# Expert weights of a hybrid decoder layer: two 1 MB pieces of one matrix by one 2 MB transfer

## The chip, the cores and the metric

The kernel runs on one core of one Trainium2 chip. The metric is the device time of one execution in microseconds. TensorE multiplies, ScalarE and VectorE work element by element, GpSimd (POOL) issues the gathers and scatters, SyncE (SP) issues the other transfers. Each engine runs its own instructions in program order and waits on semaphores.

## The reference, cut to what matters

One decoder layer on 1024 tokens of width 1024: a combined projection, differential attention and retention, a gated merge, an output projection, and a mixture of 32 SwiGLU experts of which each token uses two. The change touches the experts alone:

```
h2 = rms_norm(x, norm2_g)                       # (1024, 1024)
for each expert e (width 512), on the rows routed to it:
    a = rows @ w_gate[e]                        # w_gate, w_up: (32, 1024, 512) float32
    u = rows @ w_up[e]
    y = (silu(a) * u) @ w_down[e]               # w_down: (32, 512, 1024) float32
    out[rows] += y * routing weight
```

The three matrices of an expert have 2 MB each, so the experts read 201 MB of weights.

## The kernel before

The stages ahead of the experts end at about 890 us. In the expert stage each expert works on one block of 128 gathered rows. All products are made as three products of parts (`split3`): each float32 operand is taken apart into a high part in float32r and the low rest. ScalarE makes the high part of a weight piece (`high_piece`, L1167), VectorE the low part (`low_piece`, L1703), and both are needed before TensorE can use the piece.

**Pieces and ring.** Each matrix of an expert comes in two pieces of 1 MB, 128 partitions with 8 KB each. So an expert has 6 pieces: c = 0 to 3 for gate and up, c = 4 and 5 for down. `PIECES` puts the 192 pieces in the order of use: the four pieces of expert e stand ahead of the two down pieces of expert e - 1. Gate and up alternate: gate first half, up first half, gate second half, up second half. The pieces go through a ring of 10 slots of 16 KB per partition, of which the loaded piece fills the first 8 KB (the low part replaces it there) and the high part the other 8 KB. Each slot has a semaphore `w_land0` to `w_land9` for the landing. `load_piece` on SP waits until the piece that was in the slot ten pieces earlier is used:

```
if q >= N_SLOTS:
    sp.wait_ge(S["w_used"], q - N_SLOTS + 1)
```

TensorE raises `w_used` after the 12 matmuls of each piece (`gate_up`, `down`). The loads are all issued on SP, first pieces 0 to 3 amid the stores of the stage before, then the others in one loop once the first expert's rows have landed.

**Order on the engines**, for expert e (the 32 experts in order of use, `expert_at` says which one it is):

- TensorE: four pieces of gate and up for e; turn the rows of expert e + 1 (`turn_x`, L562); two down pieces of e - 1; turn the hidden rows of e (L562).
- ScalarE: silu of e (`gate_silu`, L1180); high part of the next rows (`x_high`, L1171); high parts of pieces (e + 1, 1) and (e + 1, 2); high part of the turned hidden rows (L1175); high parts of (e + 1, 3), (e, 4), (e, 5) and (e + 2, 0).
- VectorE: hidden rows of e, silu times up (`hidden`, L1779); low part of (e + 1, 0); low part of the next rows (`x_low`, L1774); low part of (e + 1, 1); the weighed result y of e - 1 (`rows_out`, L1800); low part of the hidden rows (L1783); low parts of (e + 1, 2), (e + 1, 3), (e, 4) and (e, 5).
- GpSimd: gather the rows of expert e + 3 when those of e + 2 are turned (L1335); scatter y of expert e with an addition in memory (L1343).

PSUM holds gate's product in `PROJ[0]`, up's in `PROJ[1]`. `overflow` and its blocks serve experts with more than 128 rows.

## Time and profile before

| | before |
|---|---|
| median of 3 runs | 1505.51 us (1505.3 to 1505.54) |
| the profiled execution | 1504.28 us |
| its span, first to last instruction | 1502.3 us |
| TensorE busy, share of the span | 1431.3 us, 95% |
| VectorE busy | 1015.5 us, 68% |
| ScalarE busy | 768.6 us, 51% |
| GpSimd busy | 387.9 us, 26% |
| transfers | 282.68 MB, mean 188 GB/s |
| mean granted TensorE clock, share of full speed | 0.988 |

The profile is of one execution. Times count from the first instruction's start. Busy shares are averages over stages that differ, so the expert stage has to be looked at by itself, by windows, timelines and the chain of waits, which follows the work that ended last back from step to step. In timelines a merged row (xN) covers all its instructions from the first start to the last end.

### The profile page before, as it was taken

How to read it: one execution, taken by the hardware profiler on the slowest of the kernel's cores; microseconds unless marked ns; L12 is line 12 of the kernel's file. 1: busy time of each engine (PE TensorE's matmuls, PEld its weight loads, DVE VectorE, ACT ScalarE, POOL GpSimd, SP SyncE). 2: the span in 40 equal slices, each digit the busy share in tenths (PEclk: the TensorE clock that was granted, in tenths of full speed). 3: DMA queues.
4: the chain of work that ended last, by engine and by line, in shares of the span. 5: the costliest groups of instructions: out<-in, count | busy, mean ns of one | idle time of the engine just before them, and what ended most of it. 6: DMA issues, size and time to landing. Idle time of an engine off the chain costs nothing.

```text
span 1502.3 us, 19200 instructions
## 1 busy us (share of the span) xinstructions
PE 1431.3 (95%) x7296; PEld 1198.4 (80%) x7297; DVE 1015.5 (68%) x1433; ACT 768.6 (51%) x1091; POOL 387.9 (26%) x448
## 2 busy tenths in 40 slices
PE   5899999999999999999999969999999999999995
PEld 4788888888888788888888858888888787777784
DVE  6855655664664433434332876999999999999994
ACT  5643453453453322333232446767777777777772
POOL 2325325424424300000001421333332222222221
PEclk9999999999999999999999979999999999999998
DMA  7011010110210333453341469999999999999991
GB/s 227 13 43 45 17 43 11 51 42 2 60 43 1 85 84 89 122 144 85 84 189 57 169 234 377 362 373 376 375 378 375 374 367 364 367 370 368 365 347 49
DMA packets 129996, 282.68 MB, mean 188 GB/s; under 512 B 15728, under 2 KB 94704, under 8 KB 105328
## 3 DMA queue, kind: packets, MB, share of 16 engines
q1 hardware_dynamic: 119216, 264.31, 48.8%
q0 software_dynamic: 9216, 16.81, 4.5%
q8 instruction: 60, 0.98, 0.3%
q10 hardware_dynamic: 1472, 0.32, 0.1%
q14 instruction: 32, 0.26, 0.1%
HBM read 273.00 MB, written 25.17 MB: 198 GB/s over the span
## 4 chain that ended last, share of the span: by engine, by line
PE 72%; DMA 14%; DVE 6%; issue 2%; ACT 2%; POOL 2%; POOLq 0%; DVEq 0%; ACTq 0%
PE proj L105 14%; PE proj L107 14%; PE proj L106 13%; DMA w_slot<-in_w_up 9%; PE scores L105 5%; PE scores L107 5%; PE scores L106 5%; DMA w_slot<-in_w_gate 4%; PE outs L751 2%; PE scores L684 2%; DVE w_low L1703 2%; ACT w_high L1167 1%; PE turned L105 1%; PE turned L107 1%; PE turned L106 1%
## 5 line engine op out<-in xcount | busy, mean ns | idle before, releaser
L1703 DVE TENSOR_TENSOR w_low<-w_slot,w_high 128x2048 fp32r<-128x2048 f32 x192 | 434.4, 2285 | 11.1 <-ACT w_high L1167 10.0
L1167 ACT ACTIVATE w_high<-w_slot 128x2048 fp32r<-128x2048 f32 x190 | 359.6, 1914 | 106.7 <-DMA w_slot<-in_w_gate 40.8
L105 PE MATMUL proj<-w_high,xeH 128*128 128x512 f32 x512 | 206.2, 403 | 11.5 <-DVE w_low L1703 8.7
L107 PE MATMUL proj<-w_high,xeL 128*128 128x512 f32 x512 | 201.3, 393 | 0.0
L106 PE MATMUL proj<-w_low,xeH 128*128 128x512 f32 x512 | 201.2, 393 | 0.0
L1343 POOL DMA_INDIRECT out<-y,ids_rows x32 | 107.1, 3347 | 228.9 <-DVE y L1800 228.9
L105 PEld LDWEIGHTS proj<-w_high,xeH 128*128 128x128 f32 x512 | 97.2, 190 | 38.9 <-DVE w_low L1703 16.3
L975 ACT ACTIVATE wCH<-wC_in 128x1024 fp32r<-128x1024 f32 x48 | 47.6, 1052 | 154.4 <-DMA wC_in<-in_w_branch_b 154.4
L1398 DVE TENSOR_TENSOR wCL<-wC_in,wCH 128x1024 fp32r<-128x1024 f32 x48 | 56.9, 1237 | 91.3 <-ACT wCH L975 91.3
L107 PEld LDWEIGHTS proj<-w_high,xeL 128*128 128x128 f32 x512 | 97.1, 190 | 21.3
L1335 POOL DMA_INDIRECT xe<-h_rows,ids_rows x32 | 54.8, 1711 | 225.9 <-PE scores L562 213.4
L106 PEld LDWEIGHTS proj<-w_low,xeH 128*128 128x128 f32 x512 | 97.2, 190 | 18.9
L105 PE MATMUL proj<-wBH,hTH 128*128 128x512 f32 x256 | 111.5, 436 | 0.0
L105 PE MATMUL scores<-w_high,hidH 128*128 128x512 f32 x256 | 103.4, 404 | 4.9 <-DVE w_low L1703 4.9
L105 PE MATMUL proj<-wAH,hTH 128*128 128x384 f32 x256 | 97.7, 382 | 5.7 <-DVE wAL L1393 4.2
L107 PE MATMUL proj<-wBH,hTL 128*128 128x512 f32 x256 | 101.1, 395 | 0.0
L107 PE MATMUL scores<-w_high,hidL 128*128 128x512 f32 x256 | 100.5, 393 | 0.0
L106 PE MATMUL proj<-wBL,hTH 128*128 128x512 f32 x256 | 100.3, 392 | 0.0
L106 PE MATMUL scores<-w_low,hidH 128*128 128x512 f32 x256 | 100.2, 391 | 0.0
L107 PE MATMUL proj<-wAH,hTL 128*128 128x384 f32 x256 | 86.5, 338 | 0.0
L106 PE MATMUL proj<-wAL,hTH 128*128 128x384 f32 x256 | 86.2, 337 | 0.0
L105 PEld LDWEIGHTS scores<-w_high,hidH 128*128 128x128 f32 x256 | 48.6, 190 | 14.1 <-issue 5.1
(277 smaller groups left out, 3080.5 us busy)
## 6 DMA issues: line engine op xcount, KB each, us to landing
w_slot<-in_w_gate SPq DMA_DIRECT2D x64, 1024.0 KB, 21.1
w_slot<-in_w_up SPq DMA_DIRECT2D x64, 1024.0 KB, 22.2
w_slot<-in_w_down SPq DMA_DIRECT2D x64, 1024.0 KB, 21.1
wC_in<-in_w_in SPq DMA_DIRECT2D x32, 512.0 KB, 4.9
wB_in<-in_w_in SPq DMA_DIRECT2D x16, 512.0 KB, 6.4
wA_in<-in_w_in SPq DMA_DIRECT2D x12, 512.0 KB, 5.8
x_all<-in_x SPq DMA_DIRECT2D x4, 1024.0 KB, 8.7
wC_in<-in_w_branch_a SPq DMA_DIRECT2D x16, 256.0 KB, 5.6
```

Source lines behind the costliest of these rows:

```text
L105: pe.matmul(out, lh, rh, start=start, stop=False)
L106: pe.matmul(out, lh, rl, start=False, stop=False)
L107: return pe.matmul(out, ll, rh, start=False, stop=stop)
L684: pe.matmul(SC[:, c, t0 * 128:t1 * 128], q_part[r, 0, :], k_part[r, 1 + t0:1 + t1, :].rearrange("p a b -> p (a b)"), start=q_part is qkTH ...
L751: last = pe.matmul(OB[:, 0:128], aT[:, j, :], V[:, j, :], start=(j == 0), stop=(j == i2))
L975: act.activation(wCH[sub][:, piece * 8:piece * 8 + 8, :], wC_in[sub][:, piece * 8:piece * 8 + 8, :], ACT.Copy).then_inc(S["wC_high"], 1)
L1167: act.activation(w_high[slot][:], w_in6[slot][:], ACT.Copy).then_inc(S["w_split"], 1)
L1335: pool.indirect_dma_start(out=xe[:], out_offset=None, in_=h2_dram, in_offset=bass.IndirectOffsetOnAxis(ap=ids_rows[:, expert_at(j):expert_ ...
L1343: pool.indirect_dma_start(out=out_rows, out_offset=bass.IndirectOffsetOnAxis(ap=ids_rows[:, expert_at(j):expert_at(j) + 1], axis=0), in_=y ...
L1398: dve.tensor_tensor(wCL[sub][:, r, :], wC_in[sub][:, r, :], wCH[sub][:, r, :].bitcast(F32), ALU.subtract).then_inc(S["wC_low"], 1)
L1703: dve.tensor_tensor(w_low[slot][:], w_in6[slot][:], w_high[slot][:].bitcast(F32), ALU.subtract).then_inc(S["w_lows"], 1)
```

## The change

The order of use within an expert becomes gate, gate, up, up, down, down, so that neighbouring pieces are the two halves of one matrix. Where such a pair lies in slots 0 and 1, 4 and 5, 6 and 7 or 8 and 9, `load_pair` issues one transfer of 2 MB: 128 partitions, per partition 16 KB in a row of the source, put down as two runs of 8 KB that lie 16 KB apart. It waits until both slots are used. Both halves then have one semaphore, so the high part of either half waits for both. Slots 2 and 3 (`ALONE`) don't lie side by side, and there the pair stays two transfers of 1 MB. To make the other slots neighbours, slots 3 to 7 get other places in memory. Pieces 0 and 1, loaded ahead, are one pair; 2 and 3 are loaded one by one at the places where they were. As gate is whole after piece 1, `gate_silu` waits for piece 1 instead of 3, and `hidden` waits for piece 3 itself. For expert 0, whose rows come in two halves, the second half is wanted at piece 1 instead of 2.

```diff
--- before.py
+++ after.py
@@ -36,6 +36,8 @@
 NO_ROW = 1024
 N_SLOTS = 10
 N_GROUPS = 4
+ALONE = (2, 3)
+BLOCK_SLOTS = (0, 1, 2, 4, 5, 6)
 
 
 def expert_at(j):
@@ -48,6 +50,11 @@
     if c < 4:
         return max(6 * e - 2, 0) + c
     return min(6 * e + 8, 6 * N_EXP - 2) + c - 4
+
+
+def land_of(slot):
+
+    return f"w_land{slot if slot in ALONE else slot - slot % 2}"
 
 
 PIECES = sorted((use_of(e, c), e, c) for e in range(N_EXP) for c in range(6))
@@ -318,9 +325,11 @@
         key_w = [ro(f"key_w{i}", [P, 256]) for i in range(2)]
 
 
-        slot_at = [R_HT, R_HT + 16 * KIB, R_WORK, R_B, R_B + 16 * KIB, R_OT, R_OT + 16 * KIB, merged_at[1],
+        slot_at = [R_HT, R_HT + 16 * KIB, R_WORK, merged_at[1], R_B, R_B + 16 * KIB, R_OT, R_OT + 16 * KIB,
                    R_HT + 32 * KIB, R_HT + 48 * KIB]
-        w_in6 = [sb(f"w_slot{i}", [P, 2048], F32, at=slot_at[i]) for i in range(N_SLOTS)]
+        w_pairs = {i: sb(f"w_pair{i}", [P, 2, 4096], F32, at=slot_at[i]) for i in range(0, N_SLOTS, 2) if i not in ALONE}
+        w_in6 = [sb(f"w_slot{i}", [P, 2048], F32, at=slot_at[i]) if i in ALONE else w_pairs[i - i % 2][:, i % 2, 0:2048]
+                 for i in range(N_SLOTS)]
         w_low = [sb(f"w_low{i}", [P, 2048], F32R, at=slot_at[i]) for i in range(N_SLOTS)]
         w_high = [sb(f"w_high{i}", [P, 2048], F32R, at=slot_at[i] + 8 * KIB) for i in range(N_SLOTS)]
         xe = sb("xe", [P, 1024], F32, at=R_A)
@@ -372,7 +381,7 @@
             wC_landed1 wC_high wC_low oT_high oT_low gates_done ys_done sig_tanh sig_mul merged_step
             wD_landed0 wD_landed1 wD_high wD_low mH mL d_done x2_done g2_in router_in wrg_done n2_sq n2_rstd h2_gained h2_done x2T_done x2T_out lg_done logit_done h2_stored0 h2_stored1 masks_out
             route_step place_step before_done pos_mm rows_mm
-            weight_exps x0_T x0_H x0_L tables_done w_land0 w_land1 w_land2 w_land3 w_land4 w_land5 w_land6 w_land7 w_land8 w_land9 w_used
+            weight_exps x0_T x0_H x0_L tables_done w_land0 w_land2 w_land3 w_land4 w_land6 w_land8 w_used
             w_split w_lows idx_copied xe_landed xeT_done xeH_done xeL_done silu_done hid_done hidT_done
             hidH_done hidL_done y_out scattered0 scattered1 scattered2 scattered3 x2_stored cur_landed rows_weighed head_consts xe_zero v_w v_hi v_lo""".split()
         S = {n: sem(n) for n in names}
@@ -504,17 +513,31 @@
             sp.wait_ge(S["ys_done"], N_UNITS)
             sp.dma_start(wD_in[1][:], wo_v[:, :, 512:1024]).then_inc(S["wD_landed1"], DMA)
 
-            def load_piece(q):
+            def source(e, c):
+
+                return (wg_v, wg_v, wu_v, wu_v, wd_v, wd_v)[c][e]
+
+            def load_one(q):
                 _, j, c = PIECES[q]
-                e = expert_at(j)
                 if q >= N_SLOTS:
                     sp.wait_ge(S["w_used"], q - N_SLOTS + 1)
-                v, at = ((wg_v, wu_v)[c % 2], c // 2) if c < 4 else (wd_v, c - 4)
-                sp.dma_start(w_in6[q % N_SLOTS][:], v[e][:, at * 2048:at * 2048 + 2048]).then_inc(S[f"w_land{q % N_SLOTS}"], DMA)
+                at = c % 2 * 2048
+                sp.dma_start(w_in6[q % N_SLOTS][:], source(expert_at(j), c)[:, at:at + 2048]).then_inc(S[land_of(q % N_SLOTS)], DMA)
+
+            def load_pair(q):
+                _, j, c = PIECES[q]
+                slot = q % N_SLOTS
+                if slot in ALONE:
+                    load_one(q)
+                    load_one(q + 1)
+                else:
+                    if q >= N_SLOTS:
+                        sp.wait_ge(S["w_used"], q - N_SLOTS + 2)
+                    sp.dma_start(w_pairs[slot][:, :, 0:2048], source(expert_at(j), c).rearrange("p (a b) -> p a b", a=2)
+                                 ).then_inc(S[land_of(slot)], DMA)
 
             sp.wait_ge(S["d_done"], 8)
-            load_piece(0)
-            load_piece(1)
+            load_pair(0)
 
             def store_h2(i):
                 sp.wait_ge(S["h2_done"], i + 1)
@@ -526,28 +549,26 @@
             for i in range(4):
                 store_h2(i)
                 store_x2(i)
-            load_piece(2)
+            load_one(2)
             for i in range(4, N_TILES - 1):
                 store_h2(i)
                 store_x2(i)
             sp.wait_ge(S["d_done"], 16)
-            load_piece(3)
+            load_one(3)
             store_h2(N_TILES - 1)
             store_x2(N_TILES - 1)
             sp.wait_ge(S["xe_landed"], DMA)
-            for q in range(4, 6 * N_EXP):
+            for q in range(4, 6 * N_EXP, 2):
                 if q == 8:
                     sp.wait_ge(S["x2_stored"], N_TILES * DMA)
-                load_piece(q)
+                load_pair(q)
 
             sp.wait_ge(S["tables_done"], 2)
 
             def loads_again(n, e, b):
                 sp.wait_ge(S["scattered0"], n * DMA + DMA * (N_EXP // N_GROUPS))
-                for c in range(4):
-                    sp.dma_start(w_in6[c][:], (wg_v, wu_v)[c % 2][e][:, (c // 2) * 2048:(c // 2) * 2048 + 2048]).then_inc(S["v_w"], DMA)
-                for c in (4, 5):
-                    sp.dma_start(w_in6[c][:], wd_v[e][:, (c - 4) * 2048:(c - 4) * 2048 + 2048]).then_inc(S["v_w"], DMA)
+                for c in range(6):
+                    sp.dma_start(w_in6[BLOCK_SLOTS[c]][:], source(e, c)[:, c % 2 * 2048:c % 2 * 2048 + 2048]).then_inc(S["v_w"], DMA)
 
             for g in range(N_GROUPS):
                 sp.wait_ge(S[f"scattered{g}"], DMA * (N_EXP // N_GROUPS))
@@ -565,8 +586,8 @@
         def gate_up(pe, c, slot):
 
             for k in range(4):
-                kk = (c // 2) * 4 + k
-                last = split3(pe, PROJ[c % 2][:, :], (xeH[:, kk, :], xeL[:, kk, :]),
+                kk = (c % 2) * 4 + k
+                last = split3(pe, PROJ[c // 2][:, :], (xeH[:, kk, :], xeL[:, kk, :]),
                               (w_high[slot][:, k * 512:(k + 1) * 512], w_low[slot][:, k * 512:(k + 1) * 512]),
                               kk == 0, kk == 7)
             return last
@@ -913,7 +934,7 @@
                     pe.wait_ge(S["w_lows"], q + 1)
                     if e == 0 and c == 0:
                         pe.wait_ge(S["x0_L"], 1)
-                    if c == (2 if e == 0 else 0):
+                    if c == (1 if e == 0 else 0):
                         pe.wait_ge(S["xeL_done"], e + 1)
                     gate_up(pe, c, q % N_SLOTS).then_inc(S["w_used"], 1)
 
@@ -953,12 +974,12 @@
                 pe.wait_ge(S["xeL_done"], n + (N_EXP + 1))
                 pe.wait_ge(S["v_lo"], n * 6 + 6)
                 for c in range(4):
-                    gate_up(pe, c, c).then_inc(S["w_used"], 1)
+                    gate_up(pe, c, BLOCK_SLOTS[c]).then_inc(S["w_used"], 1)
                 pe.wait_ge(S["hid_done"], n + (N_EXP + 1))
                 turn_rows(pe, hid, TB, 4, 4).then_inc(S["hidT_done"], 1)
                 pe.wait_ge(S["hidL_done"], n + (N_EXP + 1))
                 for c in (4, 5):
-                    down(pe, c, c).then_inc(S["w_used"], 1)
+                    down(pe, c, BLOCK_SLOTS[c]).then_inc(S["w_used"], 1)
                 pe.wait_ge(S["y_out"], n + (N_EXP + 1) + FREE)
 
             overflow(pe, block_products, all_tables)
@@ -1153,7 +1174,7 @@
                     act.wait_ge(S["late_in"], DMA)
                     act.activation(count_masks[:], consts_late[0][:, 0:256], ACT.Copy).then_inc(S["masks_out"], 1)
                 if cnt in (9, 10):
-                    high(w_high[cnt - 9][:], w_in6[cnt - 9][:], S[f"w_land{cnt - 9}"], DMA, S["w_split"])
+                    high(w_high[cnt - 9][:], w_in6[cnt - 9][:], S[land_of(cnt - 9)], DMA, S["w_split"])
                 if cnt >= 8:
                     i = cnt - 8
                     act.wait_ge(S["n2_rstd"], 2 * i + 3)
@@ -1163,7 +1184,7 @@
 
             def high_piece(q):
                 slot = q % N_SLOTS
-                act.wait_ge(S[f"w_land{slot}"], DMA * (q // N_SLOTS + 1))
+                act.wait_ge(S[land_of(slot)], DMA * (q // N_SLOTS + 1))
                 act.activation(w_high[slot][:], w_in6[slot][:], ACT.Copy).then_inc(S["w_split"], 1)
 
             def x_high(value):
@@ -1175,7 +1196,7 @@
                 act.activation(hidH[:].rearrange("p a b -> p (a b)"), TB[:, :], ACT.Copy).then_inc(S["hidH_done"], 1)
 
             def gate_silu(e):
-                act.wait_ge(S["w_used"], use_of(e, 3) + 1)
+                act.wait_ge(S["w_used"], use_of(e, 1) + 1)
                 act.wait_ge(S["hid_done"], e)
                 act.activation(silu[:], PROJ[0][:, :], ACT.Silu).then_inc(S["silu_done"], 1)
 
@@ -1207,7 +1228,7 @@
 
             def block_steps(n, e, b):
                 act.wait_ge(S["v_w"], n * (6 * DMA) + 6 * DMA)
-                for c in range(6):
+                for c in BLOCK_SLOTS:
                     act.activation(w_high[c][:], w_in6[c][:], ACT.Copy).then_inc(S["v_hi"], 1)
                 x_high(n + (N_EXP + 1))
                 act.wait_ge(S["w_used"], n * 6 + (6 * N_EXP + 4))
@@ -1774,8 +1795,9 @@
                 dve.tensor_tensor(xeL[:].rearrange("p a b -> p (a b)"), SC[:, 0, :],
                                   xeH[:].rearrange("p a b -> p (a b)").bitcast(F32), ALU.subtract).then_inc(S["xeL_done"], 1)
 
-            def hidden(value):
+            def hidden(value, used):
                 dve.wait_ge(S["silu_done"], value)
+                dve.wait_ge(S["w_used"], used)
                 dve.tensor_tensor(hid[:], silu[:], PROJ[1][:, :], ALU.mult).then_inc(S["hid_done"], 1)
 
             def hid_low(value):
@@ -1804,7 +1826,7 @@
                 low_piece(use_of(1, c))
             for e in range(N_EXP):
                 more = e + 1 < N_EXP
-                hidden(e + 1)
+                hidden(e + 1, use_of(e, 3) + 1)
                 if more:
                     if e:
                         low_piece(use_of(e + 1, 0))
@@ -1825,11 +1847,11 @@
             rows_out(N_EXP - 1)
 
             def block_lows(n, e, b):
-                for c in range(6):
-                    dve.wait_ge(S["v_hi"], n * 6 + (c + 1))
+                for i, c in enumerate(BLOCK_SLOTS):
+                    dve.wait_ge(S["v_hi"], n * 6 + (i + 1))
                     dve.tensor_tensor(w_low[c][:], w_in6[c][:], w_high[c][:].bitcast(F32), ALU.subtract).then_inc(S["v_lo"], 1)
                 x_low(n + (N_EXP + 1))
-                hidden(n + (N_EXP + 1))
+                hidden(n + (N_EXP + 1), n * 6 + (6 * N_EXP + 4))
                 hid_low(n + (N_EXP + 1))
 
             for g in range(N_GROUPS):
```

## Rows read from the trace of the kernel before

**Rows 1.** The page: mean busy tenths of the 16 DMA engines in 40 slices.

```profile
DMA  7011010110210333453341469999999999999991
```

**Rows 2.** Windows: stretch, its us; busy us by engine; granted clock, DMA share, GB/s.

```profile
900.00:910.00 10.00, 10.00 (x67) 9.06 (x66) 2.06 (x2) 0.99 (x3) 0.00 (x0) 1.00 1.01 422
915.00:920.00 5.00, 5.00 (x18) 3.94 (x17) 5.00 (x3) 5.00 (x4) 0.00 (x0) 0.77 0.87 327
950.00:1130.00 180.00, 180.00 (x852) 150.71 (x851) 170.32 (x103) 133.50 (x92) 62.77 (x21) 1.00 1.01 374
1150.00:1450.00 300.00, 291.62 (x1352) 238.43 (x1350) 275.35 (x162) 215.14 (x146) 73.98 (x33) 1.00 0.99 369
```

**Rows 3.** DMA, 1150 to 1450 us: packets, MB, share; issues, us to landing.

```profile
q1 hardware_dynamic: 13974, 101.75, 87.9%
...
out<-y,ids_rows POOLq DMA_INDIRECT x17, 12.1
```

**Rows 4.** Chain of waits from 1430 us: start us, us, what.

```profile
1430.61 0.50 PE proj L105
...
1436.38 23.04 DMA w_slot<-in_w_up
1459.45 1.93 ACT w_high L1167
...
1463.61 1.28 DVE y L1800
...
1467.74 0.50 PE proj L105
...
1478.92 0.48 PE turned L562 x4
```

**Rows 5.** DMA of the whole span: a queue of small packets; 2 MB issues.

```profile
q10 hardware_dynamic: 1472, 0.32, 0.1%
...
wD_in<-in_w_out SPq DMA_DIRECT2D x2, 2048.0 KB, 13.4
```

**Rows 6.** ScalarE's timeline at expert 31: start us, us, what [idle before].

```profile
1454.78 1.91 ACT L1167 ACTIVATE w_high<-w_slot 128x2048 fp32r<-128x2048 f32 x1 [0.83 <-DMA w_slot<-in_w_gate]
1456.60 0.58 ACT L1180 ACTIVATE silu<-proj 128x512 f32<-128x512 f32 x1
1457.08 1.02 ACT L1171 ACTIVATE xeH<-scores 128x1024 fp32r<-128x1024 f32 x1
...
1461.93 1.92 ACT L1167 ACTIVATE w_high<-w_slot 128x2048 fp32r<-128x2048 f32 x1 [0.57 <-DMA w_slot<-in_w_gate]
```

**Rows 7.** SP's timeline: DMA issues, merged where xN.

```profile
889.46 0.33 SPq L513 DMA_DIRECT2D w_slot<-in_w_gate  x1
...
916.58 3.49 SPq L513 DMA_DIRECT2D w_slot<-in_w_down  x2
...
1446.14 9.16 SPq L513 DMA_DIRECT2D w_slot<-in_w_down  x4
```

**Rows 8.** VectorE's timeline, second half of the first expert's rows.

```profile
892.12 0.69 DVE L1789 TENSOR_TENSOR xeL<-scores,xeH 128x512 fp32r<-128x512 f32 x1 [0.16 <-ACT xeH L1189]
```

**Rows 9.** ScalarE's timeline at the second piece issued near 890 us.

```profile
897.13 1.92 ACT L1167 ACTIVATE w_high<-w_slot 128x2048 fp32r<-128x2048 f32 x1 [0.55 <-DMA w_slot<-in_w_up]
```

**Rows 10.** VectorE's timeline at expert 31.

```profile
1457.21 0.69 DVE L1779 TENSOR_TENSOR hid<-silu,proj 128x512 f32<-128x512 f32 x1 [0.94 <-ACT silu L1180]
1457.82 2.28 DVE L1703 TENSOR_TENSOR w_low<-w_slot,w_high 128x2048 fp32r<-128x2048 f32 x1
1460.02 1.22 DVE L1774 TENSOR_TENSOR xeL<-scores,xeH 128x1024 fp32r<-128x1024 f32 x1
...
1464.80 0.68 DVE L1783 TENSOR_TENSOR hidL<-turned,hidH 128x512 fp32r<-128x512 f32 x1
```

**Rows 11.** Chain of waits: turning an expert's rows on TensorE.

```profile
960.71 0.88 PE scores L562 x8
```

**Rows 12.** DMA, 900 to 910 us: the weights' queue.

```profile
q1 hardware_dynamic: 576, 4.20, 100.6%
```

## Prediction

> I call the 6 pieces (1 MB each) of expert j in order of use (j, 0) to (j, 5); (j, 4) and (j, 5) are the down pieces, used one expert late. Piece n of the stream lies in ring slot n mod 10.
>
> **What bounds the kernel now.** I read the page's slices first, to find where transfers take over [rows 1]: the DMA engines are full only from slice 24, that is from about 890 us. Until then nothing that the diff touches sets the pace. The windows then split the expert stage [rows 2]. From 950 to 1130 us TensorE is busy 180.00 of 180 us: it is the bound, while the transfer engines are also full (share 1.01). From 1150 to 1450 us TensorE is idle 8.4 of 300 us and the DMA share is 0.99: now data sets the pace. Both halves fit together: the 10-slot ring is a store that a slightly faster TensorE empties until it is used up between 1130 and 1150 us, and from then on each expert waits for bytes. Every us in which the transfer engines idle, even at 915 us, is therefore paid for at the end.
>
> Two more facts of the same views. With nothing beside them the pieces stream at 422 GB/s, in the data-bound half all traffic together makes 369 [rows 2]; there the weights' queue takes 87.9% of the engines' time [rows 3]. And a piece takes some 23 us from issue to landing [rows 4], about eight pieces' worth of queue.
>
> The chain of waits says what of a landing reaches the end [rows 4]. The last transfer in it was issued at 1436.38 when TensorE released a slot, and its piece, (31, 1), is taken up by ScalarE at 1459.45. From there: high part, y of expert 29, low part of (31, 2), TensorE from 1467.74, then without a gap (31, 2), (31, 3), down of expert 30 to 1478.92, and a tail to 1502.3 that is fixed work. So (31, 2) starts 1467.74 - 1459.45 = 8.29 us after (31, 1) has landed. Call that landing T; the remaining 34.6 us behind 1467.74 do not depend on how pieces arrive, since (31, 4) and (31, 5) wait for the hidden rows.
>
> **The change, part by part.**
>
> *Number of transfers.* 192 pieces are 96 pairs; every fifth begins in slot 2 and stays two transfers (19), so 77 transfers fall away. Bytes, 8 KB runs and their number stay. What goes is 77 issues on SP (0.33 us each, on a queue that idles: nothing) and one tiny completion packet per engine and transfer. The nearest row is queue 10 with 1472 packets of 0.32 MB in 0.1% of 16 x 1502 us [rows 5]: 24 us / 1472 = 16 ns. So 77 x 16 ns = 1.3 us is the most to gain and 0 the least; I take -0.6 us.
>
> *Rate of a 2 MB transfer.* The nearest rows are one piece after the other at 422 GB/s [rows 2], and the 2 MB transfers of wD_in, 13.4 us to landing [rows 5], but those go in 2 KB rows behind other loads. The pair keeps 8 KB runs, so I take the first and change nothing; the other end is a rival below. The Trainium skill, page "DMA: Bandwidth & Descriptors", section "Bandwidth", speaks for the change: it says to batch to 1 MiB or more and measures 341 GB/s at 1 MB against 425 at 16 MB. By it a 2 MB transfer would be several per cent faster than a 1 MB one; the row at 422 GB/s shows that queued 1 MB pieces are already there, so the trace does not bear it out.
>
> *Order gate, gate, up, up.* The PSUM bank of gate is complete two pieces sooner, so silu may start sooner. It stands on ScalarE behind the high part of (j+1, 0), and in the data-bound half that is what it waits for (high from 1454.78, silu at 1456.60 [rows 6]), not TensorE. In the TensorE-bound half nobody on TensorE waits for it. 0 us. The new wait of VectorE's hidden product on piece 3 is met when silu is done (SP's last issue, the release by (30, 3), is at 1446.14 + 9.16 - 0.33 = 1454.97 [rows 7], before silu even started). For expert 0 the second half of xe is wanted after one piece instead of two; the second half is ready at 892.12 + 0.69 = 892.8 [rows 8], and the first piece, which starts after the first half, runs 2.7 us or more. 0 us.
>
> *The wait for two used slots.* The SP queue now issues a pair when its second slot is free. While the queue is 22 us deep this only thins it. But at 915 us it is thin: (1, 4) was issued at 916.58 and (1, 5) at 916.58 + 3.49 - 0.33 = 919.74 [rows 7], and the engines already dip to 0.87 between 915 and 920 us [rows 2]. Now both go at 919.74. Two pieces issued into an idle queue at 889.46 had both landed when ScalarE took the second at 897.13, 7.67 us later [rows 7, 9], so the pair lands at 927.4. Before, (1, 5) alone went at 919.74, one piece less behind it: 1.05 MB at 422 GB/s is 2.48 us, so it landed near 924.9. That is 2.5 us lost to the stream; at least 0 (if TensorE's releases move), at most the 3.16 us of later issue. I take +2.0.
>
> *Both halves land together.* This is the main term. (31, 0) used to land 4.67 us before (31, 1) (1454.78 and 1459.45 [rows 4, 6]); ScalarE used that time for high(31, 0), silu and xeH. Now all three stand behind T. With pitches from the rows (high 1.82, silu 0.48, xeH 0.92 [rows 6]; hid 0.61, low 2.20, xeL 1.13 to 1.22, hidL 0.60 [rows 10]; y 1.19 [rows 4, 10]) the new order is, from T: high(31, 0) to 1.85; silu to 2.4; hid 2.45 to 3.06; low(31, 0) to 5.26; xeL to 6.4; low(31, 1) to 8.6 (its high part runs 3.3 to 5.2); y to 9.8; hidL to 10.4 (hidH at 7.5 is ready); low(31, 2) to 12.6; TensorE on (31, 2) at 12.65. Against 8.29 that is +4.36 us. TensorE offers no cover. The cycle is (1467.74 - 1430.61) / 2 = 18.57 us [rows 4]. If (30, 2) started 12.65 after the landing before, then (30, 2), (30, 3) and two down pieces (1478.92 - 1467.74 = 11.18), the turns of xe (0.88 [rows 11]) and hid (0.48 [rows 4]) bring TensorE to (31, 0) at 12.65 + 12.54 - 18.57 = T + 6.6, by when xeL is there; two pieces later it is at T + 12.1 and waits 0.5 us for low(31, 2). The same page of the Trainium skill, section "Why a DMA increments its semaphore by 16 and not by 1", has the rule behind it: only the full count says that data has landed, so no half of a pair can be used sooner.
>
> *The scatter that moves along.* The 4.67 us between two landings that are otherwise 2.48 apart (1459.45 to 1461.93 [rows 4, 6]) is other traffic in between: the scatter, 12.1 us from issue to landing [rows 3]. y now comes 4.4 us later relative to the stream, so its burst can fall behind the landing T. That takes back between 0 and 4.67 - 2.48 = 2.2 us; I take -1.5.
>
> **Sum:** -0.6 + 2.0 + 4.4 - 1.5 = +4.3 us, with ends -1.3 + 0 + 4.4 - 2.2 = +0.9 and 0 + 3.2 + 4.4 - 0 = +7.6. The profiled execution took 1504.28 us (span 1502.3), so its sum is 1508.6; the median of the runs is 1505.51, 1.2 above, so I forecast 1509.8 us.
>
> **Rivals.**
>
> (a) *Faster.* Larger transfers suffer less from gather and scatter. In the data-bound half weights cost 0.879 x 16 x 300 us / 101.75 MB = 41.5 engine-us per MB [rows 3], alone 1.006 x 160 / 4.20 = 38.3 [rows 12]. Over 201.3 MB that excess is 3.2 x 201.3 / 16 = 40 us. If pairs win back an eighth, my +4.3 is cancelled; from a fifth on the kernel is measurably faster; a quarter gives 1499.8 us. For it: a switch between queues may come half as often. The section "Bandwidth" of the Trainium skill named above speaks for this case. Against it: bytes, runs and memory traffic are the same. Chance 0.11.
>
> (b) *No change.* The stagger is absorbed: the scatter burst moves wholly behind T, the start gap is closed by slots that TensorE releases in time, giving +0.9 to +3, about 1507.5 us. For it: the negative ends above are real mechanisms. Against: ScalarE's in-order queue, where high(31, 0) stands ahead of silu, leaves 4.4 us that nothing hides. Chance 0.22.
>
> (c) *Much slower.* TensorE has only 0.5 us of slack per expert in my schedule. If the pair makes the cycle itself 0.5 us longer than 18.57, the 17 experts between 1140 and 1459 us pay 8.5 us more: 1518 us. A pair that streams worse than two pieces ends there too. Against: 20 us of queue is left above the 4.4 us that it loses. Chance 0.07.
>
> **How the numbers follow.** Forecast 0.60 (1508.6 to 1513.5), (a) 0.11, (b) 0.22, (c) 0.07. 0.2% is 3.0 us, about what a measurement of this kernel can tell from no change. Slower by more: 0.60 + 0.07 = 0.67; within: 0.22; faster: 0.11. For 8 in 10 the range takes the forecast and most of (b), from 1504.0, to 1514.0 us.
>
> **What would show it.** In the profile after: 77 issues of 2048 KB; windows at 900 to 910 us still near 422 GB/s; a deeper dip of the DMA share at 915 to 930; in the data-bound half ScalarE takes two high parts per landing and VectorE waits for silu longer than before; share still 0.98 to 1.00; the chain again through a landing of (31, 0/1), but some 12.5 us from it to TensorE on (31, 2), and that start near 1472 us. I am wrong if the weights' cost per MB falls below 41 engine-us, if the landing of (31, 0/1) moves by more than 3 us, or if silu does not stand behind the landing.

## The result and the profile after

The changed kernel takes 1519.59 us (median of 4 runs, 1519.48 to 1520.29) against 1505.4 us before, measured beside it (4 runs, 1504.74 to 1505.54): ratio 1.0099, 95% interval 1.0087 to 1.0111. So it is slower, as forecast, but by 14.2 us and not by 4.3. The span of the profiled execution is 1517.8 us against 1502.3, so 15.5 us are to be found.

The windows of the kernel after, which answer to [rows 2] (stretch, its us; busy us by engine; granted clock, DMA share, GB/s):

```profile
900.00:910.00 10.00, 10.00 (x67) 9.01 (x65) 5.18 (x3) 4.74 (x5) 0.00 (x0) 1.00 1.01 419
915.00:920.00 5.00, 5.00 (x21) 4.09 (x20) 5.00 (x3) 5.00 (x3) 0.00 (x0) 0.88 0.66 270
950.00:1130.00 180.00, 175.93 (x826) 146.18 (x825) 161.71 (x96) 125.38 (x88) 52.50 (x20) 1.00 0.98 365
1150.00:1450.00 300.00, 289.59 (x1336) 239.28 (x1335) 267.18 (x158) 203.81 (x140) 73.20 (x33) 0.98 0.97 362
```

With the queue full, from 900 to 910 us, a 2 MB transfer streams as two of 1 MB did (419 against 422 GB/s). The dip at 915 us is deeper (0.66 against 0.87). The news is in the last two rows. TensorE, without a gap from 950 to 1130 us before, now idles 4.07 us there; and the transfer engines, which the forecast kept at 0.98 to 1.00 of their time, do 0.97 between 1150 and 1450 us and 2% less work. What a megabyte costs them shows in the DMA view of that stretch (queue: packets, MB, share of 16 engines; issues, KB each, us to landing), which answers to [rows 3]:

```profile
q1 hardware_dynamic: 13089, 99.74, 85.1%
...
w_pair<-in_w_gate SPq DMA_DIRECT2D x13, 2048.0 KB, 18.8
...
out<-y,ids_rows POOLq DMA_INDIRECT x16, 12.4
```

0.851 x 16 x 300 us / 99.74 MB is 40.95 engine-us (time summed over the 16 engines) per MB, against 41.5 before. So weights don't cost more of the engines' time: the engines have nothing to do for 3% of it, and that though a transfer still takes 18.8 us from issue to landing.

The chain of waits after, which answers to [rows 4] (start us, us, what):

```profile
1430.56 20.46 DMA w_pair<-in_w_gate
1451.06 1.80 issue
1452.86 0.59 ACT silu L1201
1453.47 0.69 DVE hid L1801
1454.16 2.06 DVE w_low L1724
1456.28 1.23 DVE xeL L1795
1457.64 0.47 PE proj L112
...
1459.87 0.43 PE proj L113
...
1499.02 0.76 PE scores L112
```

The chain goes through a landing, one high part (listed as 1.80 us of "issue"), silu, hid, low, xeL, and then TensorE: the queue that the forecast described, with silu behind the landing. But it stops TensorE in mid-stage, at expert 30, where the forecast let the queue cover it. TensorE's timeline shows what it waited for there, and when it begins (31, 2), 24 matmuls of 0.23 us after the start of expert 31 at 1477.02:

```profile
1457.64 0.47 PE L112 MATMUL proj<-w_high,xeH 128*128 128x512 f32 x1 [2.49 <-DVE xeL L1795]
...
1482.60 0.39 PE L112 MATMUL proj<-w_high,xeH 128*128 128x512 f32 x1
```

From 1455 us back to 1075 us there are five such stops of 2.3 to 2.7 us, all released by xeL, one at every fifth expert (ten slots and six pieces per expert fall together again every 30 pieces). Behind three of the five the granted clock falls. The windows of the kernel after around these places, and at the end:

```profile
1268.00:1274.00 6.00, 5.47 (x13) 4.33 (x14) 6.00 (x5) 6.00 (x5) 1.40 (x1) 0.50 0.91 365
1363.00:1367.00 4.00, 3.76 (x10) 2.98 (x11) 4.00 (x5) 4.00 (x4) 0.00 (x0) 0.57 0.91 370
1459.00:1462.00 3.00, 3.00 (x9) 2.33 (x8) 3.00 (x4) 3.00 (x3) 0.29 (x1) 0.50 0.99 412
1497.00:1503.00 6.00, 3.98 (x10) 3.14 (x11) 4.07 (x2) 1.34 (x1) 0.30 (x1) 0.50 0.24 33
```

0.50 is the lower level, 1.2 GHz, at which a matmul of the chain above takes 0.43 us instead of 0.23. In the kernel before no such stretch lies between 917 and 1483 us.

ScalarE's timeline after at expert 31, which answers to [rows 6]:

```profile
1467.45 1.93 ACT L1188 ACTIVATE w_high<-w_pair 128x2048 fp32r<-128x2048 f32 x1 [2.58 <-DMA w_pair<-in_w_gate]
1469.28 0.58 ACT L1201 ACTIVATE silu<-proj 128x512 f32<-128x512 f32 x1
1471.35 1.03 ACT L1192 ACTIVATE xeH<-scores 128x1024 fp32r<-128x1024 f32 x1 [1.50 <-PE scores L583]
1472.28 1.91 ACT L1188 ACTIVATE w_high<-w_pair 128x2048 fp32r<-128x2048 f32 x1
1475.16 1.92 ACT L1188 ACTIVATE w_high<-w_pair 128x2048 fp32r<-128x2048 f32 x1 [0.98 <-DMA w_pair<-in_w_up]
```

**Where 15.5 us went.** T, the landing of (31, 1), moved from 1459.43 to 1467.43: **+8.0**. From T to TensorE on (31, 2) it was 8.3 us and is 15.2 (1482.60): **+6.9**. From there to the end it is 35.2 instead of 34.6 us: **+0.6**. The forecast had -0.1, +4.4 and 0 for the three (its other terms lie in T). The low part of (31, 2) is not what TensorE waits for in the second stretch: it is ready at 1480.8, 13.4 us after T, where 12.65 were worked out (the rest is xeH, which stands 1.50 us behind rows that TensorE delivers late). TensorE itself is behind, since its stop at expert 30 and the half clock after it, and from 1457.64 to 1494.1 it runs without a gap. So the last landing on the chain is that of (30, 0) and (30, 1) at 1451.0, one expert before T. The first question of the experiments is why the landings move by 8 us and more.

### The profile page after: what moved, and what is told of

It reads as the page before. It is cut to its first block, busy times and chain, and to the rows that moved or that the text cites. A ratio compares the mean times of both kernels' runs of the same rounds, so it can differ in the third digit from the quotient of the medians.

```text
span 1517.8 us, 19155 instructions
## 1 busy us (share of the span) xinstructions
PE 1437.4 (95%) x7296; PEld 1205.4 (79%) x7297; DVE 1013.4 (67%) x1433; ACT 760.7 (50%) x1091; POOL 380.1 (25%) x448
## 4 chain that ended last, share of the span: by engine, by line
PE 72%; DMA 13%; DVE 8%; issue 2%; POOL 2%; ACT 1%; SPq 0%; POOLq 0%; DVEq 0%; ACTq 0%
PE proj L112 14%; PE proj L114 14%; PE proj L113 14%; DMA w_pair<-in_w_gate 11%; PE scores L112 5%; PE scores L114 5%; PE scores L113 5%; DVE w_low L1724 3%; PE outs L772 2%; PE scores L705 2%; DMA w_pair<-in_w_up 1%; PE turned L112 1%; PE turned L114 1%; PE turned L113 1%; PE scores L583 1%
## 5 line engine op out<-in xcount | busy, mean ns | idle before, releaser
L1188 ACT ACTIVATE w_high<-w_pair 128x2048 fp32r<-128x2048 f32 x152 | 287.2, 1912 | 141.5 <-DMA w_pair<-in_w_gate 63.3
L1724 DVE TENSOR_TENSOR w_low<-w_pair,w_high 128x2048 fp32r<-128x2048 f32 x154 | 346.9, 2285 | 15.5 <-ACT w_high L1188 15.4
L1364 POOL DMA_INDIRECT out<-y,ids_rows x32 | 97.4, 3044 | 230.4 <-DVE y L1822 230.4
L1724 DVE TENSOR_TENSOR w_low<-w_slot,w_high 128x2048 fp32r<-128x2048 f32 x38 | 85.8, 2284 | 0.0
## 6 DMA issues: line engine op xcount, KB each, us to landing
w_slot<-in_w_gate SPq DMA_DIRECT2D x12, 1024.0 KB, 18.6
```

What stands on the lines that cost most here:

```text
L1188: act.activation(w_high[slot][:], w_in6[slot][:], ACT.Copy).then_inc(S["w_split"], 1)
L1364: pool.indirect_dma_start(out=out_rows, out_offset=bass.IndirectOffsetOnAxis(ap=ids_rows[:, expert_at(j):expert_at(j) + 1], axis=0), in_=y ...
L1724: dve.tensor_tensor(w_low[slot][:], w_in6[slot][:], w_high[slot][:].bitcast(F32), ALU.subtract).then_inc(S["w_lows"], 1)
```

## The experiments

Each expectation speaks of its rivals by name. "One" in a diff is the kernel after with single transfers for all ten slots, each with its own landing semaphore; diffs are against it unless said otherwise. Ratios are to the kernel before, run on the same chip beside it; 0.1% is 1.5 us.

**The change in its parts: order, joint landing, late issue.** The order of use and the places of the slots alone:

```diff
-ALONE = (2, 3)
+ALONE = tuple(range(10))        # every piece one 1 MB transfer
```

> The new order gate, gate, up, up and the new places of the slots, with ten single 1 MB transfers as before. If order and places cost nothing (what the prediction says), within 0.2% of before: 1505.4 +- 1.5 us. If the earlier silu or the new places matter, 2 us or more off.

Measured: 1503.07 us, ratio 0.9994 (0.9984 to 1.0003). Order and places cost nothing.

The joint landing alone: ScalarE waits for both halves, each issued as soon as its slot is free.

```diff
                 act.wait_ge(S[land_of(slot)], DMA * (q // N_SLOTS + 1))
+                if slot not in (2, 3):
+                    act.wait_ge(S[land_of(slot ^ 1)], DMA * (q // N_SLOTS + 1))
```

> Single transfers, each issued as soon as its own slot is used, but ScalarE waits for both halves of a pair (except in slots 2 and 3). It isolates the joint landing. The prediction's main term says +4.4 us, less what the scatter gives back: 1508 to 1510. Rival (the late issue alone empties the transfer engines): less than +3 us here, since the stream is issued as early as slots allow.

Measured: 1509.59 us, 1.0036 (1.0025 to 1.0048), about 5.4 us. T is at 1457.32 us, where the order alone has it (1457.38); all the cost stands behind T, 50.4 us to the end instead of 44.0. It has the stops of 2.1 to 2.7 us and stretches at half clock too, the last stop right behind the landing of (30, 1), and TensorE begins (31, 2) 15.5 us after T. So it is these that the joint landing brings, and they don't move the data.

The late issue alone: both halves go when the second slot is free, as two transfers with a landing each.

```diff
-                    sp.wait_ge(S["w_used"], q - N_SLOTS + 1)
+                    sp.wait_ge(S["w_used"], q - N_SLOTS + (1 if q % N_SLOTS in (2, 3) else 2 - q % 2))
```

> Single transfers with landings of their own, but both halves of a pair are issued only when both slots are used. It isolates the late issue. The prediction says +2 us (only the gap at 915 us): 1507.5. Rival: the stream is thin throughout, because the slowest of the 16 engines lags pieces behind the others, so late issue idles engines again and again: +6 to +9 us, 1511 to 1514.

Measured: 1514.53 us, 1.0067 (1.005 to 1.0084), about 10 us. T moves by 12.5 us against the order alone (1469.9), and 43.3 us follow it. This is the part that I had priced at the dip near 915 us alone.

Both together, still as transfers of 1 MB:

> Late issue and joint landing together, still as two 1 MB transfers. It leaves of the change only the size of the transfer out. If the size of the transfer costs nothing: like the changed kernel, 1519.6 +- 2 us. If the 2 MB transfer itself is what costs: nearer to 1511 to 1513, with the rest of the 14 us due to the size.

Measured: 1517.14 us, 1.0089 (1.007 to 1.0109). The kernel after is at 1.0099 (1.0087 to 1.0111), so no cost of the transfer's size is shown: the two differ by some 1.5 us, less than their intervals leave open.

**silu ahead of the landing.** In the kernel after, the high part of (e + 1, 0) moves behind silu:

```diff
+                    if e:
+                        high_piece(use_of(e + 1, 0))
                     x_high(e + 2)
...
                 high_piece(use_of(e, 5))
-                if e + 2 < N_EXP:
-                    high_piece(use_of(e + 2, 0))
```

> The changed kernel, with ScalarE's silu ahead of the high part of (e+1, 0) instead of behind it. If the joint landing costs because ScalarE's queue blocks silu, this takes 1 to 4 us back (1515 to 1518.5). If it costs only because the first half is there later, nothing changes (within 1 us of the changed kernel).

Measured: 1517.26 us, 1.0095 (1.0078 to 1.0112): no gain that can be told, though the intervals would hide one of 2 to 3 us. From 950 to 1480 us TensorE's waits for xeL fall from 15.2 to 7.2 us and those for low parts rise from 3.8 to 11.5: behind the same late landing another instruction takes the wait.

**Where in time the late issue costs.** Late only from piece 60 on, long after the dip at 915 us:

```diff
-... + (1 if q % N_SLOTS in (2, 3) else 2 - q % 2))
+... + (1 if q < 60 or q % N_SLOTS in (2, 3) else 2 - q % 2))
```

> As the late issue alone, but only from piece 60 on; the first 60 are issued as early as before. It takes the gap at 915 us out. If the late issue costs throughout: +7 to +8 us of the +10. If it costs at 915 us, as the prediction said: 0 to +2.

Measured: 1512.21 us, 1.0061 (1.0045 to 1.0078), against 1.0067 for the whole. The dip at the start is worth about 1 us of the 10, no more than the intervals leave open anyway; the loss goes on all the time.

**Is it the thinner queue?** In the kernel before, every piece from the tenth on is issued one use of TensorE later, then two, then three (the last in "one"):

```diff
-                    sp.wait_ge(S["w_used"], q - N_SLOTS + 1)
+                    sp.wait_ge(S["w_used"], q - N_SLOTS + 2)    # 3 and 4 in the others
```

> The kernel before with one edit: every piece from the tenth on is issued one use later, as if the ring had 9 slots. If the stream is thin (about 3 pieces of data in the engines, though 7 have not landed), every issue 2.7 us later idles the fast engines: +8 us or more. If 23 us of queue is really there, at most +3 us, from the start at 915 us.

> The kernel before, every piece from the tenth on issued two uses later (8 slots' worth of ring). Gives the price of lateness without pairing: one use later was +3.8. If the engines' backlog of about 3 pieces is the store, two later is steeper than twice: +9 us or more; if it is linear, +7.

> Order alone, every piece three uses late, none issued together (7 slots' worth of ring). No piece is sooner than in the issue by four. If lateness counts little and the interval much: +6 to +8 us, far below the issue by four. If lateness is what costs there: more than the issue by four.

Measured: 1.0025 (1.0015 to 1.0034), 1.0033 (1.002 to 1.0045) and 1.0046 (1.003 to 1.0063), so 3.8, 5.0 and 7.0 us. One use later for all 182 pieces costs well under half of what it costs in the late issue, where only four pieces of ten go later. The first two fit neither side of their expectations (3.8 us against at most 3 or at least 8, and 5.0 against 7 or 9), the third fits. So a thinner queue has a price, but it isn't the answer.

**Is it the pairs?** First the same lateness spaced out: the odd piece of a pair goes one use later as well, so that no piece goes earlier than in the late issue.

```diff
-... + (1 if q % N_SLOTS in (2, 3) else 2 - q % 2))
+... + (1 if q % N_SLOTS in (2, 3) else 2))
```

> As the late issue alone, but the odd piece of each pair is issued one use later as well, so that no two are issued together; slots 2 and 3 as before. No piece is issued sooner than in the late issue. If lateness is what costs: +10 us or more. If two issues at once are what costs (engines run dry in the doubled interval between them): back to +2 to +5 us.

> The late issue alone once more, beside the three above on the same chip: +10 us, 1.005 to 1.0085 of before.

Measured, on one chip: spaced 1508.01 us, 1.0023 (1.0014 to 1.0033); in pairs again 1514.03, 1.0064 (1.0045 to 1.0082). Issuing four more pieces of every ten later wins 6 us back. SP's timelines show the difference; in pairs (late issue alone) and then spaced, a merged x2 covering both issues and what lies between:

```profile
1382.32 0.81 SPq L525 DMA_DIRECT2D w_slot<-in_w_down  x2
1388.62 0.80 SPq L525 DMA_DIRECT2D w_slot<-in_w_gate  x2
1394.98 0.81 SPq L525 DMA_DIRECT2D w_slot<-in_w_up  x2
```

```profile
1383.89 3.97 SPq L525 DMA_DIRECT2D w_slot<-in_w_gate  x2
1390.26 3.57 SPq L525 DMA_DIRECT2D w_slot<-in_w_up  x2
1396.22 3.92 SPq L525 DMA_DIRECT2D w_slot<-in_w_down  x2
```

In pairs no new data is asked for during some 5.5 to 6 us. The windows of the data-bound half, one row each from the late issue (pairs), the spaced one, and the two and three uses of lateness:

```profile
1150.00:1450.00 300.00, 285.95 (x1323) 233.66 (x1322) 270.08 (x159) 212.32 (x144) 71.29 (x32) 1.00 0.97 361
```

```profile
1150.00:1450.00 300.00, 289.35 (x1346) 237.57 (x1346) 273.25 (x161) 214.24 (x144) 75.10 (x32) 1.00 1.00 366
```

```profile
1150.00:1450.00 300.00, 290.58 (x1349) 237.75 (x1348) 275.54 (x162) 216.06 (x146) 72.39 (x32) 1.00 1.00 367
```

```profile
1150.00:1450.00 300.00, 290.96 (x1349) 238.02 (x1349) 274.58 (x162) 215.26 (x145) 72.90 (x32) 1.00 1.00 367
```

The DMA share (before the GB/s) is 0.97 with pairs (0.96 in the repeat) and 1.00 with every spacing, however late. The 0.2 to 0.5% that lateness alone costs does not show in this share. Then more of the bunching: the pieces of slots 2 and 3 in pairs as well (`+ 2 - q % 2`), and all pieces by fours (`+ 4 - q % 4`).

> As the late issue alone, but the pairs in slots 2 and 3 are issued together too. If issuing two at once costs: more than the late issue's +10, about 5/4 of it, +12 to +13 us. If the irregular place of slots 2 and 3 is what costs: less than +10.

> Order alone, but pieces are issued by four, when the fourth slot is used: the first three are 3, 2 and 1 uses late. If the interval between issues is what costs (now 11 us and more against 5 us for two), far more than the pairs' +9 to +10: +20 us or more. If only lateness counts (mean 1.5 uses): +4 to +5, by the rows of 9 and 8 slots.

Measured: 1513.0 us, 1.0059 (1.0039 to 1.0078), share 0.97, not more than for the four pairs of five, where 12 to 13 us were expected; and 1519.16 us, 1.0104 (1.0086 to 1.0122), share 0.95. By fours no piece goes later than in the run with three uses of lateness (1.0046), yet it costs twice as much; the expected 20 us it doesn't reach.

**Two requests together, or a doubled interval?** Each piece by two transfers issued back to back, at the interval of the kernel before. First split by partitions, then by columns:

```diff
-                sp.dma_start(w_in6[q % N_SLOTS][:], source(expert_at(j), c)[:, at:at + 2048]).then_inc(...)
+                for half in (slice(0, 64), slice(64, 128)):
+                    sp.dma_start(w_in6[q % N_SLOTS][half, :], source(expert_at(j), c)[half, at:at + 2048]).then_inc(...)
```

```diff
+                for a in (0, 1024):
+                    sp.dma_start(w_in6[q % N_SLOTS][:, a:a + 1024], source(expert_at(j), c)[:, at + a:at + a + 1024]).then_inc(...)
```

> Order alone, with every piece loaded as two transfers of 512 KB (64 partitions each, the same 8 KB runs), issued one behind the other at the piece's own time. If two issues back to back are what costs, as such: +5 us or more. If it is the doubled interval between issues (engines run dry in it): within 0.2% of before, since interval and bytes stay.

> The order alone, with each 1 MB piece loaded by two transfers of 512 KB issued one behind the other: each covers all 128 partitions and half of the columns (4 KB in a row per partition). A piece is requested as soon as its slot is used, as in the kernel before; only two requests follow each other without a pause and the number of transfers doubles. Theory 'doubled interval' (requests in pairs cost 9 to 10 us because no new data is requested for two uses of TensorE, 5 us, in which the transfer engines that are ahead run dry): the interval stays 2.5 us, so no more than 2 to 3 us slower, for twice the transfers, and a transfer share of 0.99 to 1.00 between 1150 and 1450 us. Rival 'back to back' (two requests that arrive together disturb each other in the queue, whatever the interval): as much as the pairs cost, 8 us or more, share near 0.97. Should 4 KB per partition stream slower by themselves, the window 900 to 910 us shows it (422 GB/s with 8 KB).

Measured: 1884.2 us, 1.2519 (1.2467 to 1.2571), and 1521.96 us, 1.0118 (1.0101 to 1.0135). Neither fits its expectation, and each first has to be read in the window with the queue full. Split by partitions, then by columns:

```profile
900.00:910.00 10.00, 9.68 (x65) 8.67 (x64) 3.77 (x3) 4.57 (x4) 0.03 (x1) 1.00 1.03 212
```

```profile
900.00:910.00 10.00, 10.00 (x68) 9.10 (x66) 2.63 (x2) 1.70 (x3) 0.00 (x0) 1.00 1.02 406
...
1150.00:1450.00 300.00, 285.01 (x1302) 234.43 (x1303) 266.25 (x158) 209.16 (x141) 78.13 (x31) 0.98 0.99 357
```

With 64 partitions per transfer the engines are busy all the time and move half as much; the run says nothing on the question. By columns they move 406 GB/s instead of 422 and are busy 0.99 of the time in the data-bound half. Its DMA view from 1150 to 1450 us:

```profile
q1 hardware_dynamic: 27121, 98.75, 88.5%
```

0.885 x 4800 / 98.75 = 43.0 engine-us per MB against 41.5, over 201.3 MB and 16 engines 19 us: what a byte costs in this form is enough for the whole loss of some 17 us. Its time alone would have been read as the rival's, and its share of 0.99 speaks for the doubled interval. But the run is no clean test: the engines had more to do per piece, and an issue took SP 1.06 us (median) instead of 0.33, so that the second request came about 1.1 us behind the first and not 0.37 as in the late issue.

**Engine by engine.** What idles can be read from the landings themselves. Every landing, of 1 MB or 2 MB, is counted in sixteen steps, and the trace keeps the time of each; I take each step as one of the 16 transfer engines being done with its part. In the runs of the table below the first steps, the second steps and so on always come in the order of issue, as they would if each engine works through its requests in order. In the kernel before (1150 to 1450 us, medians) a piece's first step comes 5.2 us after its issue, the eighth 6.3, the twelfth 18.6 and the last 22.3. So half of the engines have at most two pieces before them, and the 22 us are the backlog of the others.

An engine has run dry when its step of the last request is in. How long the early half waits then can be estimated: the time from the step to the next issue, plus 2 us (in the kernel before no piece had its first step sooner than 4.5 us after its issue, and it streams in 2.5 us). Idle share of the eight earliest steps so estimated, 1150 to 1450 us:

| run | share, % | run | share, % |
|---|---|---|---|
| before | 1.8 | late issue (pairs) | 10.9 |
| order alone | 1.9 | the same again | 11.2 |
| one, two, three uses late | 2.9, 2.7, 2.5 | slots 2 and 3 in pairs too | 9.6 |
| spaced | 4.8 | by fours | 15.4 |
| joint landing alone | 3.6 | the kernel after | 7.7 |

For the latest four steps it is 0.0 in every one of these runs. So the doubled interval idles the engines that are ahead, and lateness without it hardly does. It also fits that slots 2 and 3 in pairs too cost nothing more. What stays open is the last link: a landing waits for its latest engine, and the latest ones never ran dry. Why they too get through their parts more slowly when the early ones burst and pause, no run here shows.

**An earlier start of the loads.** Pieces 4 and up don't wait for the first expert's rows:

```diff
-            sp.wait_ge(S["xe_landed"], DMA)
+            sp.wait_ge(S["tables_done"], 1)
```

> Single transfers in the new order, and piece 4 and those behind it are issued when the row table is done (about 884 us) and no longer when the first expert's rows have landed (889.5 us). If each us of idle transfer engines in the expert stage is paid at the end: -3 to -5 us against the order alone. Rival: the gather is slowed by the weights, or TensorE's start sets the end: 0 or slower.

Measured: 1508.67 us, 1.0035 (1.0021 to 1.005), slower. TensorE's timeline gives the reason:

```profile
894.30 0.91 PE L954 MATMUL scores<-consts,xe 128*128 128x128 f32 x3 [10.55 <-DMA xe<-h_rows,ids_rows]
```

The rows that TensorE needs first landed at 894.3 instead of 889.5 us, behind the weights, though their gather was issued at 885 us in both. And the ring holds no more than ten pieces: with all of them loaded the transfer engines stood nearly still until TensorE freed slots (share 0.19 from 915 to 920 us, 0.87 before).

## Why the prediction was wrong, point by point

- **The step that failed** is the one on the wait for two used slots: "While the queue is 22 us deep this only thins it", with the start gap of +2.0 as its whole price. The term measures +9 to +10 us alone (1.0067 and 1.0064), of which the start gap is about 1 (1.0061 with the late issue from piece 60 on). The gap itself was worked out well: the pair (1, 4) and (1, 5) landed at 928.1 where I had 927.4. I read 22 us from issue to landing as 22 us of work in hand; it is that for the latest of the 16 engines, and half of them have done their part after 6.3 us. When the engines idle is seen in the kernel after, in windows of 2 us around SP's issues at 1360.51 and 1370.57 us:

```profile
1360.51 0.55 SPq L536 DMA_DIRECT2D w_pair<-in_w_up  x1
1370.57 0.54 SPq L536 DMA_DIRECT2D w_pair<-in_w_down  x1
```

```profile
1366.00:1368.00 2.00, 2.00 (x9) 1.59 (x8) 2.00 (x3) 2.00 (x2) 0.69 (x1) 0.81 1.05 446
1368.00:1370.00 2.00, 2.00 (x11) 1.65 (x10) 2.00 (x2) 2.00 (x2) 2.00 (x1) 1.00 0.57 242
1370.00:1372.00 2.00, 2.00 (x11) 1.65 (x10) 2.00 (x2) 0.19 (x1) 0.75 (x1) 1.00 0.66 193
1372.00:1374.00 2.00, 2.00 (x10) 1.66 (x9) 2.00 (x2) 1.03 (x1) 0.00 (x0) 1.00 0.89 215
1374.00:1376.00 2.00, 2.00 (x11) 1.68 (x10) 1.89 (x1) 1.37 (x2) 0.00 (x0) 1.00 1.01 324
```

From 7.5 us after the last request on the share is 0.57, though that request has 12 us left to its landing (20.2 us after its issue); some 3.5 us after the next one the share is back at 1.01. The steps of the landing say which engines stand: of the request at 1360.51 the first came at 1368.8, the eighth at 1369.0 and the last at 1380.7. So eight engines had nothing left of the weights 1.5 us before the next request. Shown is that requests in pairs idle the engines that are ahead (share 0.96 to 0.97, by fours 0.95) and spaced ones, at equal or greater lateness, idle them much less (1.00). How that holds up the landings, which wait for the engines behind, is argued and not shown. The case shows too how it can feed on itself: the 10 us between these two requests hold a stop of TensorE of 2.29 us (up to 1363.2) and the half clock behind it.
- **The joint landing** had the right queue and nearly the right size, on a path that was not the binding one. Forecast were +4.4; 5.4 us were measured alone. The queue of work behind the landing ran as worked out, also at expert 30 (xeL done 6.5 us after the landing, 6.4 in the sum). But the sum laid its price on the wait of (31, 2) for its low part, and TensorE never waited there: it waited for xeL at the first piece of expert 30, and of every fifth expert before. "TensorE offers no cover" and the 0.5 us of slack worked out there pointed at it. That the size comes out so near is partly luck.
- **The scatter** that was to give 1.5 us back doesn't show: T didn't come earlier in the joint landing alone (1457.32 against 1457.38).
- **Fewer transfers** (-0.6) **and the rate of a 2 MB transfer** (0): the rate holds, 419 against 422 GB/s and 40.95 engine-us per MB. Neither term shows by itself: 1.0089 without the 2 MB transfers and 1.0099 with them can't be told apart.
- **The order** (0): right, 0.9994 (0.9984 to 1.0003).
- **The end.** The 34.6 us behind the start on (31, 2) I took over unchanged. They grew by 0.6; the half-clock stretch there lasts 6.8 us from 1496.5 where it lasted 3.4 from 1483.9, but TensorE stands still for its first 2.5 us.
- **The sum of the parts:** 5.4 + 10 = 15.4 us for the joint landing and the late issue alone, 13.4 for both together (1.0089): not far from additive, since one acts behind T and the other on T.
- **The rivals.** (a) fell: 40.95 engine-us per MB is 0.5 less than before, but the engines idle more than that saves, and the late issue with transfers of 1 MB has 41.1 too. (b) fell. (c), the much slower one, came nearest, by "the pair makes the cycle itself 0.5 us longer". My argument against it, 20 us of queue, was the same misreading. The time lies above its 1518.
- **The markers.** 77 issues of 2048 KB and silu behind the landing came as written. The share between 0.98 and 1.00 and T within 3 us did not, nor did the chain: it goes through (30, 0) and (30, 1), and (31, 2) starts at 1482.6 and not near 1472. The cost per MB, 40.95, lies just past its mark of 41. By the prediction's own terms these are the signs of the error.

No version beats the kernel before measurably; the order alone equals it.

## What to carry to other kernels

Where loads go through a ring, ask in what rhythm requests reach the queue, and not only how long a landing takes: here requesting two slots at a time cost 10 us, and requesting every one of them one, two or three uses later 4 to 7. The time from issue to landing is that of the engine furthest behind; the engines that were ahead were done 5 to 6 us after an issue, no longer than the pause that the pairs made. Merge neighbouring transfers only where the single ones lose rate, which the window with the queue full shows beforehand (here 422 GB/s at 1 MB and 419 at 2 MB, so nothing was to be won). And count what each half of a merged transfer releases on its own: every instruction that stood between the two landings moves behind the second.

## What the hardware did that was not expected

- Transfers over 64 partitions moved 212 GB/s where 128 partitions moved 422, at the same 8 KB rows and with the transfer engines busy throughout (share 1.03). The Trainium skill has the rule, and this run agrees with it: its page "SBUF — State Buffer", section "Can I just issue two DMAs to hit both halves?", says that only one transfer spanning all 128 partitions reaches all ports and that two transfers to the two halves don't add up.
- The 16 transfer engines drift apart: at 909 us the first and last were done with a piece 1.6 us apart, at 1032 us 8.5 us apart, and from 1150 to 1450 us 17 us (median).
- Rows of 4 KB, in transfers of half the size, cost 43.0 engine-us per MB, rows of 8 KB 41.5. The two causes aren't parted.
- In the kernel after, the granted clock was at 0.50 for 3.4 to 6.8 us behind three of the five stops of TensorE of 2.3 to 2.7 us, and not behind the other two; one stop of 1.9 us with the order alone and one of 2.0 us in the kernel before, at 910 us, were followed by 3.4 us at 0.50. Behind the stops of 0.6 to 1.2 us in the kernel before, the clock stayed at full speed.
- A gather that was issued while weights were being loaded landed 4.8 us later (894.3 against 889.5 us).
